# Keys before queries in a latent attention stage, and two value groups moved behind the first scores

## What is computed

```python
def mla_queries(h, wq_a, q_a_norm, wq_b, q_norm):
    cq = rmsnorm(h @ wq_a, q_a_norm)                     # rank 384
    q = (cq @ wq_b).reshape(B, S, MLA_HEADS, QK_DIM)     # 8 heads of 128 + 64
    return rmsnorm(q, q_norm)

def mla_keys_values(h, wkv_a, kv_a_norm, wkv_b, k_norm):
    kv_a = h @ wkv_a
    ckv, k_pe = kv_a[..., :KV_LORA], kv_a[..., KV_LORA:] # rank 256, shared rotary key of 64
    kv = (rmsnorm(ckv, kv_a_norm) @ wkv_b).reshape(B, S, MLA_HEADS, QK_NOPE + V_DIM)
    k_nope, v = kv[..., :QK_NOPE], kv[..., QK_NOPE:]
    k = rmsnorm(jnp.concatenate([k_nope, k_pe], axis=-1), k_norm)   # k_pe for every head
    return k, v
# the rotary parts of q and of the latent k are turned by cos/sin tables;
# o = softmax(q k^T / sqrt(192)) v over the 512 keys; x = x + gate * (o @ wo)
```

## Time and profile before

| | us |
|---|---|
| median of three runs | 1008.05 (1004.04 to 1008.82) |
| the profiled execution | 1007.38 |
| its span, first to last instruction | 1005.6 |
| TensorE busy | 951.9 (95% of the span) |
| VectorE, ScalarE, GpSimd busy | 714.9, 535.2, 300.2 |
| mean granted clock of TensorE | 0.975 of full |

### The profile page before, as it was taken

The page is one execution under the profiler, slowest core; times in us unless marked ns, Lnnn a source line. Parts: engine busy times, 40 slices in busy tenths (PEclk is TensorE's granted clock), DMA queues, the critical chain, the costliest instruction groups (busy, mean ns, idle before and its releaser), DMA issues.

```text
span 1005.6 us, 19537 instructions
## 1 busy us (share of the span) xinstructions
PE 951.9 (95%) x6890; PEld 872.8 (87%) x6890; DVE 714.9 (71%) x1135; ACT 535.2 (53%) x910; POOL 300.2 (30%) x256
## 2 busy tenths in 40 slices
PE   5998989999999999989889999999999999999995
PEld 5877556799999999968879999999999769899994
DVE  4996778677988777687886787555556873565865
ACT  3464655565665444554545566654434761674553
POOL 1942002237996111120051288631110000320022
PEclk9898999999999999999999999999999997999998
DMA  9856154169888777579525686556555232255421
GB/s 350 291 183 232 42 186 150 44 216 316 300 283 271 276 282 281 198 267 326 172 102 187 214 272 208 186 168 193 189 185 178 85 106 84 84 175 194 138 83 43
DMA packets 55341, 194.56 MB, mean 193 GB/s; under 512 B 5999, under 2 KB 8463, under 8 KB 54896
## 3 DMA queue, kind: packets, MB, share of 16 engines
q1 hardware_dynamic: 54880, 192.36, 56.0%
q0 software_dynamic: 400, 1.39, 0.4%
HBM read 192.65 MB, written 1.07 MB: 193 GB/s over the span
## 4 chain that ended last, share of the span: by engine, by line
PE 79%; DVE 12%; ACT 4%; issue 3%; DMA 1%; POOL 0%; SPq 0%; DVEq 0%; ACTq 0%
PE bank L521 23%; PE bank L522 23%; PE bank L523 22%; DVE w_lo L1550 2%; ACT w_hi L1125 1%; PE bank L783 1%; DVE products L1652 1%; PE bank L619 1%; PE bank L943 1%; DVE ada_raw L1652 1%; PE bank L774 1%; DMA x<-x_in 1%; PE bank L917 1%; PE bank L816 1%; PE bank L1035 1%
## 5 line engine op out<-in xcount | busy, mean ns | idle before, releaser
L1550 DVE TENSOR_TENSOR w_lo<-raw,w_hi 128x1024 fp32r<-128x1024 f32 (+1 forms) x261 | 340.7, 1308 | 117.3 <-ACT w_hi L1125 115.2
L1125 ACT ACTIVATE w_hi<-raw 128x1024 fp32r<-128x1024 f32 (+1 forms) x261 | 272.1, 1044 | 174.8 <-PE bank L523 166.7
L521 PE MATMUL bank<-act_hi,w_hi 128*128 128x258 f32 (+1 forms) x872 | 251.4, 288 | 0.0
L522 PE MATMUL bank<-act_lo,w_hi 128*128 128x258 f32 (+1 forms) x872 | 248.0, 284 | 0.0
L523 PE MATMUL bank<-act_hi,w_lo 128*128 128x258 f32 (+1 forms) x872 | 247.6, 284 | 0.0
L521 PEld LDWEIGHTS bank<-act_hi,w_hi 128*128 128x128 f32 x872 | 166.1, 190 | 3.3 <-issue 2.8
L522 PEld LDWEIGHTS bank<-act_lo,w_hi 128*128 128x128 f32 x872 | 166.0, 190 | 1.0 <-issue 1.0
L523 PEld LDWEIGHTS bank<-act_hi,w_lo 128*128 128x128 f32 x872 | 166.0, 190 | 0.0
L522 PE MATMUL bank<-hid_lo,w_hi 128*128 128x256 f32 x512 | 143.9, 281 | 0.0
L523 PE MATMUL bank<-hid_hi,w_lo 128*128 128x256 f32 x512 | 143.4, 280 | 0.0
L521 PE MATMUL bank<-hid_hi,w_hi 128*128 128x256 f32 x512 | 142.3, 278 | 0.0
(11 more groups left out here) (335 smaller groups left out, 1819.6 us busy)
## 6 DMA issues: line engine op xcount, KB each, us to landing
raw<-weights SPq DMA_DIRECT2D x247, 512.0 KB, 3.7
ada_raw<-ada SPq DMA_DIRECT2D x88, 512.0 KB, 4.8
raw<-weights SPq DMA_DIRECT2D x14, 384.0 KB, 4.5
ada_more<-ada SPq DMA_DIRECT2D x8, 512.0 KB, 6.0
bias<-bias_by_distance SPq DMA_DIRECT2D x1, 2048.0 KB, 9.2
x<-x_in SPq DMA_DIRECT2D x1, 1024.0 KB, 7.4
ctx<-ctx_in SPq DMA_DIRECT2D x1, 1024.0 KB, 9.4
out<-result SPq DMA_DIRECT2D x1, 1024.0 KB, 3.9
```

The source lines that it names most:

```text
L521: pe.matmul(dst, w[0], a[0], start=start, stop=False)
L522: pe.matmul(dst, w[0], a[1], start=False, stop=False)
L1125: act.activation(w_hi[:, slot, 0:width_of(c)], raw[:, slot, 0:width_of(c)], ACT.Copy).then_inc(weight_hi, 1)
L1550: dve.tensor_tensor(w_lo[:, slot, 0:w], raw[:, slot, 0:w], w_hi[:, slot, 0:w].bitcast(fp32), ALU.subtract).then_inc(weight_lo, 1)
```

## The change

**Order of stages.** The key groups come first, then the queries, then the values; the chunks are numbered and stored in that order, so keys are chunks 8 and 9, queries 10 to 15, values 16 and 17 as before.

**Keys from tiles that are not normalised.** `ckv` is split straight out of PSUM with its gain, by ScalarE and VectorE; the reciprocal over 128x512, the four normalised tiles and their splits by ScalarE and GpSimd go. Since a key is normalised afterwards anyway, its missing factor is made up elsewhere: the rotary key is multiplied with `std` (one VectorE instruction), a 65th row with `std` squared stands in for epsilon in the sums, and the values are scaled by the inverse root per token as ScalarE evacuates them. For that, four matmuls with one column (`token_std`) bring `std` into token order.

**Rotations.** The four query rotations stand behind the third pair of query groups. VectorE combines them in two `rotate_pair` calls, three instructions on 512 columns each; the key's rotation stands among the key groups. The keys' root, its reciprocal and the high and low part of that stand among the queries.

**Values and scores.** The spreads of inverse norms stand behind V2 and no longer V4, `latent_scores(0)` stands behind V5 and `latent_scores(1)` behind V6, so that V6 and V7 come after them. ScalarE has the queries' scales and an exponential on one column ahead of all evacuations of values. `convert(21)`, the chunk that follows the last value chunk, stands on VectorE ahead of the first unit's logits; the modulation rows of the units start at the third unit and end two units later.

```diff
--- before.py
+++ after.py
...
 STAGES = [
-    ("mla_in", [0] * 7 + [6]), ("q_b", [2] * 6), ("kv_b_k", [4] * 2), ("kv_b_v", [4] * 2),
+    ("mla_in", [0] * 7 + [6]), ("kv_b_k", [4] * 2), ("q_b", [2] * 6), ("kv_b_v", [4] * 2),
     ("mla_out", [1] * 8),
...
-    ("ckv", 4), ("mla_o", 8),
+    ("mla_o", 8),
...
             for a in range(4):
+                load_weights(8 + a)
                 load_ada(a)
-                load_weights(8 + a)
...
-                for g in range(6):
+                for g in (3, 4, 0, 1, 2, 5):
...
+            def token_std():
+                pe.wait_ge(lora_std, 1)
+                for tt in range(4):
+                    last = pe.matmul(bank[3][:, tt:tt + 1], std[:, tt * P:(tt + 1) * P], ident[:, 0:1],
+                                     start=True, stop=True)
+                last.then_inc(lora_sums, 1)
...
+            def key_group(h):
+                n, c = group0["kv_b_k"] + h, chunk0["kv_b_k"] + h // 4
+                pe.wait_ge(weight_lo, c + 1)
+                if h >= 2:
+                    pe.wait_ge(evacuated, n - 1)
+                for k in range(2):
+                    if h == 0:
+                        pe.wait_ge(evacuated, k + 1)
+                    last = split_product(bank[6 + h % 2][:], weight(c, (h % 4 * 2 + k) * P, P),
+                                         (ckv_hi[:, k, :], ckv_lo[:, k, :]), k == 0, k == 1)
+                last.then_inc(matmul_steps, 1)
...
+            def shared_key():
+                pe.wait_ge(kpe_by_scalar, KPE_SQUARED)
+                pe.matmul(bank[4][0:H, :], ones[0:ROPE + 1, 0:H], sq_lora[0:ROPE + 1, 2, :],
+                          start=False, stop=False).then_inc(kpe_by_tensor, 1)
+                pe.wait_ge(kpe_by_scalar, KPE_GAINED)
+                pe.wait_ge(lora_read, V_SCALE)
+                pe.matmul(bank[3][:, S:2 * S], rot, kpe[:, CTX:SC], start=True, stop=True).then_inc(kpe_by_tensor, 1)
...
-                if g >= 3:
+                if g == 3:
+                    pe.wait_ge(lora_read, V_SCALE)
+                    pe.wait_ge(kpe_by_vector, KPE_TURNED)
+                if g >= 4:
                     pe.wait_ge(evacuated, n - 3)
...
+            pe.wait_ge(const_in, 16)
+            for h in range(H):
+                key_group(h)
+                if h == 1:
+                    latent_sums()
+                if h >= 2:
+                    key_sums(h - 2)
+                if h == 4:
+                    token_std()
+                if h == 5:
+                    pe.wait_ge(rope_in, 16)
+                    shared_key()
             for i in range(6):
                 query_group(2 * i)
                 query_group(2 * i + 1)
-                if i == 0:
+                if i < 2:
+                    key_sums(H - 2 + i)
+                if i == 1:
+                    pe.wait_ge(evacuated, group0["q_b"])
                     low_rank_sums()
-                    pe.wait_ge(const_in, 16)
+                    pe.wait_ge(kpe_by_vector, KPE_SCALED)
                 if i > 0:
                     query_sums(2 * i - 2)
                     query_sums(2 * i - 1)
-                if i == 1:
-                    latent_sums()
+                if i == 2:
+                    pe.wait_ge(lora_read, Q_EPS)
+                    for p_ in range(4):
+                        last = pe.matmul(bank[6 + p_ // 2][:, (p_ % 2) * S:(p_ % 2 + 1) * S], rot, qr[:, p_, :],
+                                         start=True, stop=True)
+                    last.then_inc(rotated, 1)
             query_sums(10)
             query_sums(11)
...
-                pe.matmul(bank[5 + p_ // 2 * 2][:, (p_ % 2) * S:(p_ % 2 + 1) * S], rot, qr[:, p_, :],
-                          start=True, stop=True)
-            pe.matmul(bank[3][:, 0:S], rot, kpe[:, CTX:SC], start=True, stop=True).then_inc(rotated, 1)
...
-            pe.wait_ge(split_lo, split0["ckv"] + 4)
-            for h in range(H):
...
-                    if 4 * i + tt == 4:
+                    if 4 * i + tt == 2:
                         pe.wait_ge(k_rstd, 1)
                         pe.wait_ge(heads_ready, 1)
                         key_spread(0)
                         key_spread(1)
...
+                    if 4 * i + tt == 5:
+                        pe.wait_ge(kpe_by_vector, KPE_LOW)
+                        pe.wait_ge(q_ready, 1)
+                        pe.wait_ge(k_std, 1)
+                        pe.wait_ge(q_sums_read, 1)
+                        pe.wait_ge(lora_read, Q_EPS)
+                        latent_scores(0)
+                    if 4 * i + tt == 6:
+                        latent_scores(1)
...
-            pe.wait_ge(kpe_ready, 1)
-            pe.wait_ge(q_ready, 1)
-            pe.wait_ge(k_std, 1)
-            latent_scores(0)
-            latent_scores(1)
...
+            act.wait_ge(gqk_ready, 1)
+            for h in range(H):
+                act.wait_ge(matmul_steps, after_group[group0["kv_b_k"] + h])
+                if h >= 4:
+                    act.wait_ge(k_sums, h - 3)
+                act.activation(sq_k(h), bank[6 + h % 2][:], ACT.Square).then_inc(k_squared, 1)
+                act.activation(kn_hi[:, h, :], bank[6 + h % 2][:], ACT.Copy, scale=gqk[:]).then_inc(k_high, 1)
+                if h == 0:
+                    convert(9)
...
+                if i == 1:
+                    root(std[0:H, :], bank[4][0:H, :], QK, k_sums, H, k_std, 0.0)
...
+                if i == 2:
+                    act.wait_ge(k_inverse, 1)
+                    act.activation(k_rstd_hi[:], rstd[0:H, :], ACT.Copy).then_inc(k_rstd_high, 1)
+            act.wait_ge(qr_turned, 2)
...
+            act.wait_ge(q_std, 1)
+            act.activation(small[:, 95:96], eps[:], ACT.Exp)
             act.wait_ge(evacuated, group0["kv_b_v"])
+            act.wait_ge(lora_read, V_SCALE)
...
-                    if 4 * i + tt == 5:
+                    if 4 * i + tt == 4:
...
-                if i == 0:
-                    act.wait_ge(k_inverse, 1)
-                    act.activation(k_rstd_hi[:], rstd[0:H, :], ACT.Copy).then_inc(k_rstd_high, 1)
+                    evacuate("kv_b_v", 4 * i + tt, v_mla[:, tt, i * 512:(i + 1) * 512], width=512,
+                             scale=rstd_tok[:, tt:tt + 1])
...
+            def rotate_pair(b):
+                v, part = qr[:, 2 * b:2 * b + 2, :], tile_f32[:, 2 * b:2 * b + 2, :]
+                spread = lambda t: t.unsqueeze(1).to_broadcast([P, 2, S])
+                dve.tensor_tensor(part, bank[6 + b][:].rearrange("p (a s) -> p a s", a=2), spread(sin), ALU.mult)
+                then(dve.tensor_tensor(v, v, spread(cos), ALU.mult))
+                dve.tensor_tensor(v, v, part, ALU.add).then_inc(qr_turned, 1)
...
+            query_low(3)
+            dve.wait_ge(rotated, 1)
+            rotate_pair(0)
+            convert(16)
             query_low(5)
...
+            rotate_pair(1)
+            dve.wait_ge(k_rstd_high, 1)
+            dve.tensor_tensor(k_rstd_lo[:], rstd[0:H, :], k_rstd_hi[:].bitcast(fp32), ALU.subtract).then_inc(k_rstd, 1)
+            convert(17)
             query_low(6)
             query_low(7)
...
+            convert(18)
+            modulate(3)
+            convert(19)
             dve.wait_ge(q_sums_read, 1)
             dve.tensor_tensor(small[:, 32:48].rearrange("p (q h) -> p q h", q=2),
...
+            dve.wait_ge(qr_high, 1)
+            dve.tensor_tensor(qr_lo[:], qr, qr_hi[:].bitcast(fp32), ALU.subtract).then_inc(q_ready, 1)
             dve.wait_ge(q_std, 1)
             then(dve.reciprocal(q_scale[:, 1], q_scale[:, 0]))
             then(dve.tensor_scalar(q_scale[:, 0], q_scale[:, 1], QK ** -0.5, None, ALU.mult))
             then(dve.tensor_scalar(q_scale[:, 1], q_scale[:, 0], -1.0, None, ALU.mult))
...
+            modulate(4)
+            modulate(5)
+            convert(20)
             modulate(6)
...
             modulate(7)
...
+            convert(21)
...
-                if u < 2 * H:
-                    if u == 0:
-                        convert(21)
-                    modulate(8 + u)
+                if 2 <= u < 2 * H + 2:
+                    modulate(6 + u)
...
```

273 lines of the change are left out of this document (121 added, 152 removed).

## The result

The changed kernel is slower. Its median is 1015.9 us (1009.45 to 1018.27, seven executions), the kernel before stood at 1010.03 beside it, in seven executions of which one took 5152.51 us. That one, and three of 1171, 1842 and 4559 us among the experiments, are left out of all ratios and mean losses. The ratio is 1.0063 with a 95% interval of 1.0040 to 1.0086. I had forecast 1007.5 (1002.0 to 1012.0). The profiled execution, 1009.45 with a span of 1007.6, happens to be the shortest of its seven. On another chip, twelve executions gave 1.0067 (1.0047 to 1.0088).

A forecast was written before the change was run, and what follows sets the result against it. TensorE was taken to bound the kernel. From 1007.38 us: -11.5 + 0.8 + 2.2 + 2.8 + 3.7 + 1.65 + 0.3 = 0.0, so 1007.4, as a median 1007.5 us (range 1002 to 1012).

The forecast's parts named there:

- What bounds the kernel, what goes: TensorE bounds the stage; its six idle times (6.75 us) and two half-speed stretches (3.10, 1.65) go: -11.5 us.
- The key part: Key heads at the stage's start: they keep TensorE's pace, nothing waits for long; only token_std adds, +0.8 us.
- Rival 4: Key groups from the third on each wait 0.87 us for a low part: 5.2 us, so 1012.6; chance 0.08.
- Wait A: TensorE idle before the last query sums, until VectorE writes head 6's low part: +2.2 us (1.0 to 3.4).
- Wait C: TensorE idle before the third latent_scores, through V7's evacuation, two conversions and the logits: +3.7 us (3.4 to 4.1).
- Wait B: TensorE idle before the third value group, V2, until ScalarE evacuates V0: +2.8 us (1.5 to 3.5).
- The clock: Granted clock falling to 1.2 GHz after the new waits: charged +1.65 us at one place, +0.3 at another.
- clock behind A: Low clock during V0 and V1 shortens the wait before V2, costing nothing; what remains behind V2 costs +0.3 us.
- clock behind C: Low clock after the wait before the third latent_scores: the shorter of two earlier stretches taken, +1.65 us.
- clock behind the one-column sums: Low clock after 2 us of one-column low rank and query sums: 0 in the forecast, 1.65 us only in Rival 3.
- Rival 3: Clock stays low about 6.3 busy us after the new waits, not 3.5: 1010.2 to 1011.9 us; chance 0.19.
- Outside the stage: Before 68 us and after 192 us: nothing should move.

The follow-up runs named there:

- e_undo: Changed kernel with the values part undone (first two units' scores behind the last value group, VectorE's last conversion behind first logits), keys still first: 1.0044 of the kernel before.
- b_s7: Kernel before plus seven matmuls with sums thrown away, 2.65 us, in front of latent_values(4): 1.0010 of the kernel before.
- after_again: The changed kernel run again without any edit, for a second trace: 1.0067 of the kernel before.
- e_all: Changed kernel with low rank sums earlier, last conversions behind first logits and exp, rotated pairs sooner, queries' scales ahead of a conversion: 0.9965, second time 0.9949 of before.

## Why the prediction was wrong, step by step

**What bounds the kernel, what goes:** right for the waits. None of the six old waits is left in the changed kernel; `e_undo`, which has 1.16 and 0.36 back, shows that these belonged to the order of scores and values.

**The key part:** right but for two small waits. The key heads keep their pace with one wait of 0.39 us, and the last input projection waits 0.91 (65.67) and starts 0.42 later (before: 65.25). That later start isn't the new order's: `b_s7`, in the order of before, has the same wait (0.90, at 65.91), and the seven traces with it are just those that have no low stretch between 60 and 67 us. Rival 4 didn't come.

**Wait A** was forecast at 2.2 and is 2.37, with the pair at 1.92 against 1.9. **Wait C** was forecast at 3.7 and is 3.59, through the four links named. **Wait B** was forecast at 2.8 and is 1.12; the stretch of 1.71 in front of it covers the difference, as the part on the clock had said, and 1.12 + 1.71 is 2.83. In `after_again` the wait is 0 and the loss 3.41. I had 2.8 + 0.3 for both. My addition had a slip: its terms, 12.7 + 0.1 + 0.4 + 1.28 + 0.2 + 0.6, give 15.3 and not 15.5, so a wait of 2.6; from the end of wait A to V2 the trace has 6.71 us (119.69 to 126.40), the forecast 6.5, the terms 6.3. The table load takes 1.28 us, and its exponential starts right behind it (124.27, 125.56), so the Trainium skill's drain ("ScalarE: Activation LUTs", *What ACT_TABLE_LOAD costs*) is absent here too; the trace decides.

**The clock** is the step that failed, and the other terms show by how much. Up to the first `latent_values` of the profiled execution:

| term | forecast | trace | difference |
|---|---|---|---|
| wait A | 2.2 | 2.37 | +0.2 |
| wait B with the clock behind A | 3.1 | 2.83 | -0.3 |
| wait C | 3.7 | 3.59 | -0.1 |
| clock behind C | 1.65 | 3.41 | +1.8 |
| clock behind the one-column sums | 0 | 3.41 | +3.4 |
| later start, wait of 0.39 | 0 | 0.81 | +0.8 |
| sum | | | +5.8 |

The sum of the forecast is 0.0 there too, and the trace has +5.27 (148.19 to 153.46), so 0.5 us of the differences isn't explained by these terms. Two sentences went wrong. "After C I take the shorter of the two stretches" had one instance of each length and chose the cheaper; the longer, 3.41, came in all three traces of the changed kernel, and eight other traces show 3.4 to 8.5 us there. And the fall behind the sums stood in rival 3 alone, at 1.65 and as an addition to it, because I looked for falls behind idle time only. It came in two of three traces of the changed kernel. Rival 3 was the right mechanism, at 1010.2 to 1011.9, too small: with the 3.41 us that came behind C and behind the sums in this trace it would have been 1007.4 + 1.8 + 3.4 = 1012.6, with the mean of three traces behind the sums (1.7) 1010.9. The unplaced 3 us are on top; no step of the prediction can be named for them, and their cause stays open. The measured 1015.9 holds something else as well: the kernel before stood at 1010.03 beside it, 2 us above the 1008.05 from which I started.

**The chances** gave 0.75 to no change and 0.08 to slower. In its waits the forecast was good, in its sum it had luck. Without the clock the terms add up to +2.75 us (-6.75 + 0.8 + 2.2 + 2.8 + 3.7), where the rest rose by 0.2 (980.0 to 980.2). Of the 2.5 us between, 1.7 is the part of wait B that the slow V0 and V1 cover, which the split counts as loss. For the clock I had struck out 4.75 us in full and put 1.95 in their place, a gain of 2.8, where the mean loss rose by 6.3. The two errors have opposite signs, and the second is the larger by far. In a stage that exchanges six waits of 0.3 to 2.7 us for three of 1.1 to 3.6, nothing supported a gain there. Keeping the 4.75 us would have been the safer guess: the stage ran at full clock only in two of the four traces of the `e_all` order, whose longest wait up to the first `latent_values` is 0.91 us.

**Outside the stage** I expected no movement. The mean of the traces fits this (15.0 and 15.3) but can't exclude the unplaced 3 us, and single traces don't repeat: they differ by up to 8 us behind 200 us in one and the same order.
